# A two-layer network on one core: modulation chunks spread between the memory's products, and the attention queries' inverse root mean square put onto the scores

## The chip, the cores and the metric

The kernel runs on one core of one Trainium2 chip. It is one program that computes a whole small network from inputs in device memory. The metric is the device time of one execution in microseconds; the median of several executions is compared. The engines that matter are TensorE (PE in the profile, its weight loads PEld), VectorE (DVE), ScalarE (ACT) and SyncE (SP), whose one task here is to start the loads of the weights. A second DMA queue is fed by ScalarE.

## The reference, cut to what matters

256 latent tokens and 256 context tokens of 2048 features go through a layer with retention (8 heads), a layer with attention (16 query heads, 4 key/value heads) and a last block, which also attends to a memory. All is float32.

```
h = modulate(rms_norm(x, gain), shift, scale)     # shift, scale, gate: silu(c) @ ada_w, per layer
# memory of the last block: keys and values are products of the normed memory input
k_mem, v_mem = split(rms_norm(mem, mem_gain) @ w_mem_kv_2)
# layer 0, per head: q, k, v, g = h @ w_in ; retention ; finish(o, g) @ w_out
# layer 1:
q_l = rms_norm(heads(h @ w_q, 16, 128), q_gain)   # x * rsqrt(mean(x^2) + eps) * gain
q_l, k_l = rope_2d(q_l, row, col), rope_2d(k_l, row, col)
s = einsum(q_l, k) * scale + mask                 # over latent and context keys
y = (softmax(s, sink) @ v * silu(g)) @ w_out
```

## The kernel before, in words

**The weights.** Every weight comes from device memory once, in 936 chunks of 512 KB ([128, 1024] float32). Their order is written out by `stream_order` (L123). SyncE issues one DMA per chunk (L479) into a ring of raw slots: eight up to the first head of layer 0 (chunk 104), four from there. It issues the next one into a slot as soon as the slot's last chunk is consumed.

**Two kinds of chunk.** A *product chunk* is split in two parts: ScalarE writes `w_hi`, a rounded copy (L932), VectorE writes `w_lo = raw - w_hi` (L1413), which frees the raw slot. The product with activations, split in the same way, is three matmuls each (`product`, L506 to L508). Four pairs of `w_hi`, `w_lo` exist. A *modulation chunk* (a part of `ada_w`) is read by TensorE straight from its raw slot (L559), four chunks to a group of 256 columns of a layer's modulation; its slot is free when TensorE is done. After the fourth chunk ScalarE copies the sums out of PSUM (`ada_part`, L962), TensorE turns them (`ada_turn`, L575) and VectorE writes `mod` (`ada_add`, L1440, L1443).

**The look-ahead.** `weights_to(c)` on ScalarE and on VectorE splits up to four product chunks ahead of chunk `c`, in the order of the stream, and not past a slot whose modulation chunk comes later than `c`. ScalarE waits in it, in its own order, for the chunk's DMA and for the matmuls of four splits before.

**The order of the start.** (1) Modulation groups 0, 8, 1, 9 of layer 0. (2) `mk`: eight tiles of the memory's keys, two chunks each; after every second tile a modulation group (2, 10, 3, 11). (3) `mv`: two times eight chunks of the memory's values, with groups 4 and 12 in the first eight. (4) Groups 5 and 13, back to back. (5) `v(0)`: the value product of head 0, eight chunks of two k tiles, with the groups 6, 14, 7, 15 after its first four. For `v(0)` ScalarE and VectorE make the normed and modulated input of layer 0 on the way (`h_raws`, `h_parts`, `h_lows`), two k tiles per chunk, each of which needs the shift and scale of its group. The memory's input is normed likewise ahead of `mk`: a root and a reciprocal (`rstd`, L970, L1452), then for 16 k tiles `s_ctx` (L1546, VectorE), `h_hi` (L1028, ScalarE), `h_lo` (L1550, VectorE). (6) The heads of layer 0, with modulation chunks at each of their places by `modulation_beside`: two per place in head 0, one in the others.

**Other loads.** ScalarE's queue carries the tables (513 KB) and the memory's input (four of 512 KB) first, the tokens (four of 1 MB) at 17.8 us, and after `mv` it writes keys and values of the memory back to device memory (two of 1 MB, L1057, L1058).

**The attention.** Per key/value group (`kv`, 0 to 3) TensorE makes the gates (`az`), the scores of four heads (L738), transposes and values (L748, L757), the output product (`attn_out`), and in between the four query tiles of the next group (`aq`). The norm of a pair of query tiles is one chain: VectorE copies both tiles out of PSUM (L1724), ScalarE squares them (L1149), TensorE averages over the 128 features with a matrix of ones (L727, 512 columns), which leaves the mean in every partition, ScalarE takes the root (L970), VectorE the reciprocal of [128, 512] (L1729) and the product with gain and query (L1731); then comes the rotation (L1472 to L1475) with a swapped copy by ScalarE (L1003, L1004). VectorE adds the mask to the scores (L1752), takes the maximum (L1758), and ScalarE exponentiates.

Of the kernel before, what the change touches and what calls it, by code (L numbers as in the profile page):

```python
# [46 lines left out]
def columns(sizes):  # L47
# [16 lines left out]
def shape_constants():  # L64
# [10 lines left out]
    put("sum_parts", np.stack([p % 32 == 0, p % 32 == 1], 1))  # L75
# [25 lines left out]
def modulation_beside(h):  # L101


    places = [("t", i) for i in range(8)] + [("v", i) for i in range(8) if h < RET_HEADS - 1] + [("end",)]
    groups = [(0, n) for n in range(16, 24)] if h == 0 else [(1, n) for n in range(3 * h - 3, min(3 * h, 20))]
    chunks = [(layer, n, c) for layer, n in groups for c in range(4)]
    out, ended = {}, []
    for place in places:
        now = [chunks.pop(0) for _ in range(min(2 if h == 0 else 1, len(chunks)))]
# [6 lines left out]
BESIDE = [modulation_beside(h) for h in range(RET_HEADS)]  # L116


FIRST_GROUPS, MEM_GROUPS, LAST_GROUPS = (0, 8, 1, 9), (2, 10, 3, 11), (5, 13)
MV_GROUPS, V_GROUPS = ({3: 4, 7: 12}, {}), {0: 6, 1: 14, 2: 7, 3: 15}  # L120


def stream_order():  # L123
# [18 lines left out]
    for i in range(4):  # L142
        tile(("mk", 2 * i), "w_mem_kv_2", 2 * i * P)
        tile(("mk", 2 * i + 1), "w_mem_kv_2", (2 * i + 1) * P)
        ada(0, MEM_GROUPS[i])
    for n in range(2):
        for c in range(8):
            values(("mv", n), "w_mem_kv_2", W_M + n * 512, c)
            if c in MV_GROUPS[n]:
                ada(0, MV_GROUPS[n][c])  # L150
    for n in LAST_GROUPS:
        ada(0, n)
    for c in range(8):
        values(("v", 0), "ret_w_in", 2 * RET_Q, c)
        if c in V_GROUPS:
            ada(0, V_GROUPS[c])
# [19 lines left out]
    for c in range(8):  # L176
        values(("av",), "attn_w_in", q_w + kv_w, c)
    for h in range(GROUP):
        tile(("aq", 0, h), "attn_w_in", h * P)
    for i in range(ATTN_KV):  # L180
        tile(("ak", i), "attn_w_in", q_w + i * P)
# [90 lines left out]
class Banks:  # L272
# [42 lines left out]
    "v_set", "sink_set", "shifted", "sink_exp", "exped", "probs", "p_turned", "pv", "y_hi", "y_lo",  # L315
# [21 lines left out]
class Memory:  # L337


    def __init__(self, nc, ctx):  # L340
# [81 lines left out]
        self.sinks = sb("a_sinks", [P, GROUP])  # L422
        self.h_t1 = [self.a_s[i // 2][:, i % 2, :] for i in range(4)]
# [65 lines left out]
def tensor_program(nc, m, s):  # L489
    pe = nc.tensor  # L490
    banks = s.banks
    ident, ones_parts = m.table("ident"), m.table("sum_parts")
# [102 lines left out]
    pe.wait_ge(*s["tables_set"].at())  # L595
    ada_turn(0, 0)
    mean("mem", SIDE)
    ada(0, 1)
    ada_turn(0, 8)
    ada(0, 9)  # L600
# [1411 lines left out]
```

## Time and profile before

| | |
|---|---|
| runs | 3493.48, 3493.75, 3502.49 us; median 3493.75 |
| profiled execution | 3492.97 us, span 3491.7 us |
| TensorE busy | 3264.7 us, 93% of the span, 20298 matmuls |
| VectorE busy | 1738.8 us, 50% |
| ScalarE busy | 1260.3 us, 36% |
| DMA | 508.93 MB, mean 146 GB/s |
| places | `mk` from 61.6 us, `mv` from 117.4, `v(0)` from 190.2, head 0 from 259.0, head 1 in its `v` phase at about 440; query and key tiles of the attention 1944 to 2014, its four groups from 2038 |

Read the table as follows. TensorE is busy for most of the span, so what can be won is its idle time and the time in which its clock is granted at less than full speed. The page shows both by slices of 87 us:

```profile
PE   5979999999999999999997988987999999999998
PEclk9989999999999999999998999998999999999999
DMA  7753433333332333323243324443545444466654
```

The first three slices are the start, with TensorE idle for half of the first; the slices 23 to 27 are the attention.

### The profile page before, as it was taken

How to read it: one execution, taken by the hardware profiler on the slowest of the kernel's cores; microseconds unless marked ns; L12 is line 12 of the kernel's file. 1: busy time of each engine (PE TensorE's matmuls, PEld its weight loads, DVE VectorE, ACT ScalarE, POOL GpSimd, SP SyncE). 2: the span in 40 equal slices, each digit the busy share in tenths (PEclk: the TensorE clock that was granted, in tenths of full speed). 3: DMA queues.
4: the chain of work that ended last, by engine and by line, in shares of the span. 5: the costliest groups of instructions: out<-in, count | busy, mean ns of one | idle time of the engine just before them, and what ended most of it. 6: DMA issues, size and time to landing. Idle time of an engine off the chain costs nothing.

```text
span 3491.7 us, 47726 instructions
## 1 busy us (share of the span) xinstructions
PE 3264.7 (93%) x20298; PEld 2782.5 (80%) x20298; DVE 1738.8 (50%) x2491; ACT 1260.3 (36%) x1779; POOL 0.2 (0%) x4
## 2 busy tenths in 40 slices
PE   5979999999999999999997988987999999999998
PEld 3757677777777777777866878876999998999998
DVE  4533243434334343433436667766666555555555
ACT  3432222222222222222224454444554444444443
POOL 0000000000000000000000000000000000000000
PEclk9989999999999999999998999998999999999999
DMA  7753433333332333323243324443545444466654
GB/s 302 285 186 145 171 117 116 105 127 121 109 129 101 109 103 127 127 103 133 97 144 122 115 97 133 133 133 115 172 148 167 151 150 165 151 196 194 195 188 151
DMA packets 141635, 508.93 MB, mean 146 GB/s; under 512 B 15344, under 2 KB 19568, under 8 KB 140656
## 3 DMA queue, kind: packets, MB, share of 16 engines
q1 hardware_dynamic: 137040, 493.03, 41.5%
q10 hardware_dynamic: 4384, 12.85, 1.0%
q8 instruction: 161, 2.64, 0.3%
q14 instruction: 50, 0.41, 0.0%
HBM read 501.62 MB, written 4.19 MB: 145 GB/s over the span
## 4 chain that ended last, share of the span: by engine, by line
PE 85%; DVE 6%; DMA 3%; ACT 3%; issue 2%; SPq 0%; ACTq 0%; DVEq 0%
PE bank L506 26%; PE bank L508 25%; PE bank L507 25%; DMA raw<-stream 3%; PE bank L559 2%; PE bank L672 2%; DVE w_lo L1413 1%; PE bank L757 1%; PE bank L738 1%; PE bank L658 1%; PE bank L674 1%; DVE a_rstd L1729 1%; ACT a_s L1169 1%; PE bank L748 0%; ACT w_hi L932 0%
## 5 line engine op out<-in xcount | busy, mean ns | idle before, releaser
L506 PE MATMUL bank<-h_hi,w_hi 128*128 128x256 f32 (+1 forms) x4032 | 1269.0, 315 | 23.9 <-DVE w_lo L1413 21.6
L1413 DVE TENSOR_TENSOR w_lo<-raw,w_hi 128x1024 fp32r<-128x1024 f32 x744 | 901.5, 1223 | 695.5 <-ACT w_hi L932 690.6
L507 PE MATMUL bank<-h_lo,w_hi 128*128 128x256 f32 (+1 forms) x4032 | 1244.7, 309 | 0.0
L508 PE MATMUL bank<-h_hi,w_lo 128*128 128x256 f32 (+1 forms) x4032 | 1244.7, 309 | 0.0
L932 ACT ACTIVATE w_hi<-raw 128x1024 fp32r<-128x1024 f32 x744 | 779.1, 1057 | 1059.5 <-PE bank L508 601.5
L506 PEld LDWEIGHTS bank<-h_hi,w_hi 128*128 128x128 f32 x4032 | 762.5, 189 | 92.5 <-issue 36.8
L507 PEld LDWEIGHTS bank<-h_lo,w_hi 128*128 128x128 f32 x4032 | 763.4, 189 | 46.6 <-issue 4.9
L508 PEld LDWEIGHTS bank<-h_hi,w_lo 128*128 128x128 f32 x4032 | 761.2, 189 | 43.6
L506 PE MATMUL bank<-w_hi,h_hi 128*128 128x512 f32 x704 | 288.4, 410 | 44.9 <-DVE w_lo L1413 40.6
L508 PE MATMUL bank<-w_hi,h_lo 128*128 128x512 f32 x704 | 279.5, 397 | 0.0
L507 PE MATMUL bank<-w_lo,h_hi 128*128 128x512 f32 x704 | 279.0, 396 | 0.0
L1603 DVE SCALAR_TENSOR_TENSOR res<-bank,mod,res 128x256 f32<-128x256 f32 x320 | 134.1, 478 | 167.9 <-PE bank L508 167.9
L506 PE MATMUL bank<-o_hi,w_hi 128*128 128x512 f32 x512 | 201.6, 394 | 10.1 <-ACT vg L992 8.3
L506 PEld LDWEIGHTS bank<-w_hi,h_hi 128*128 128x128 f32 x704 | 135.1, 192 | 88.2 <-issue 51.8
L507 PE MATMUL bank<-o_lo,w_hi 128*128 128x512 f32 x512 | 200.5, 392 | 0.0
L508 PE MATMUL bank<-o_hi,w_lo 128*128 128x512 f32 x512 | 200.5, 392 | 0.0
L508 PEld LDWEIGHTS bank<-w_hi,h_lo 128*128 128x128 f32 x704 | 134.6, 191 | 29.6
L507 PEld LDWEIGHTS bank<-w_lo,h_hi 128*128 128x128 f32 x704 | 135.0, 192 | 29.0 <-issue 1.7
L559 PE MATMUL bank<-raw,cond 128*32 128x256 f32 x1536 | 119.6, 413 | 32.8 <-DMA raw<-stream 32.8
L506 PEld LDWEIGHTS bank<-o_hi,w_hi 128*128 128x128 f32 x512 | 97.0, 189 | 32.5 <-issue 12.5
L507 PEld LDWEIGHTS bank<-o_lo,w_hi 128*128 128x128 f32 x512 | 97.0, 190 | 20.0
L508 PEld LDWEIGHTS bank<-o_hi,w_lo 128*128 128x128 f32 x512 | 96.8, 189 | 20.3
(215 smaller groups left out, 2698.5 us busy)
## 6 DMA issues: line engine op xcount, KB each, us to landing
raw<-stream SPq DMA_DIRECT2D x936, 512.0 KB, 4.2
res<-tokens_in ACTq DMA_DIRECT2D x4, 1024.0 KB, 13.7
vg<-mem_in ACTq DMA_DIRECT2D x4, 512.0 KB, 10.7
res<-mem_kv ACTq DMA_DIRECT2D x2, 1024.0 KB, 10.0
out<-res SPq DMA_DIRECT2D x4, 512.0 KB, 3.0
mem_kv<-qk ACTq DMA_DIRECT2D x1, 1024.0 KB, 7.8
mem_kv<-vg ACTq DMA_DIRECT2D x1, 1024.0 KB, 11.1
tab<-tables ACTq DMA_DIRECT2D x1, 513.0 KB, 4.3
```

The lines of the kernel that those rows point to most:

```text
L506: pe.matmul(out, sh, mh, start=start, stop=False)
L507: pe.matmul(out, sh, ml, start=False, stop=False)
L508: return pe.matmul(out, sl, mh, start=False, stop=stop)
L559: mm = pe.matmul(out[32 * j:32 * j + 32, 0:L], m.cond[:, 4 * c + j, :], m.raw[SLOT[chunk]][:, j * L:(j + 1) * L], start=c == 0, stop=c == 3)
L658: mm = pe.matmul(outs[mt][:, :], m.qk[:, 2 + dt, L + mt * P:L + (mt + 1) * P], m.qk[:, dt, :], start=dt == 0, stop=dt == 1)
L672: pe.matmul(out[:, :], m.v[:, 2 + mt, dv], m.s_ctx[:, mt, :], start=mt == 0, stop=mt == 1)
L674: mm = pe.matmul(out[:, LAT], m.v[:, mt, dv], m.s_lat[:, mt, :], start=False, stop=mt == 1, skip_group_check=True)
L738: mm = pe.matmul(out[:, at - a0:at - a0 + n], q[:, qs], k, start=i == 0, stop=i == len(pairs) - 1)
L757: mm = pe.matmul(out[:, LAT], v, pt[:, kt, :], start=kt == 0, stop=kt == len(tiles) - 1)
L932: act.activation(m.w_hi[n % SLOTS][:, :], m.raw[SLOT[raw]][:, :], ACT.Copy).then_inc(s.hi, 1)
L1413: dve.tensor_tensor(m.w_lo[slot][:, :], m.raw[SLOT[raw]][:, :], m.w_hi[slot][:, :].bitcast(F32), ALU.subtract).then_inc(s.lo, 1)
L1603: i = dve.scalar_tensor_tensor(out=m.res[:, tile, cols], in0=psum(*what)[:, cols], scalar=m.mod[layer][:, 2 * KT + tile, side:side + 1], i ...
```

## The change

It has two parts that do not touch each other.

**The start.** `modulation_beside` now takes a list of places with a count of chunks at each, and the start uses it too: only the groups 0 and 8 come ahead of `mk`; the other 14 groups (56 chunks) lie two, three or five at a time behind each tile of `mk`, each second chunk of `mv` and the first five chunks of `v(0)`, so that no four chunks of a group need be neighbours. Head 0 has its 32 chunks nearly as before, the last place now without one. The small matrix `sum_parts`, which `ada_turn` needs, moves from the tables into the parameters, and the tables, the rotation of layer 0 and both writes of the memory (3 MB in all with them) are issued by ScalarE in `v(0)` behind its third chunk (c = 2). The tokens are issued one MB at a time. VectorE no longer has `ada_add(0, 8)` between the memory's `rstd` and its first `s_ctx`. In `v(0)`, `weights_to` comes ahead of `h_parts` (ScalarE) and `h_lows` (VectorE). In the heads, `o_rstd`'s reciprocal and the normed output stand one place apart (c = 1, c = 2).

**The attention.** The key tiles come ahead of the query tiles of group 0. The queries' norm is taken apart: VectorE multiplies each query tile by the gain as it leaves PSUM (`q_in`), ScalarE squares the tile from PSUM (`q_square`), the rotation follows at once. `q_means` is eight matmuls per group, each with the squares of 128 tokens of a head as the stationary side and one column of ones as the moving side, so that the means lie with a token per partition, [128, 8] for all four heads; root and reciprocal are taken of that. The result is multiplied onto the scores of the token, in the instruction that adds the mask. For group 0 these stand behind its gates, for the others in the third pair of `attn_out` of the group before. ScalarE loads its function tables 30 times where it was 28, the two more in group 0.

```diff
-FIRST_GROUPS, MEM_GROUPS, LAST_GROUPS = (0, 8, 1, 9), (2, 10, 3, 11), (5, 13)
-MV_GROUPS, V_GROUPS = ({3: 4, 7: 12}, {}), {0: 6, 1: 14, 2: 7, 3: 15}
+FIRST_GROUPS = (0, 8)
+BESIDE = {"start": modulation_beside(
+    [(("mk", i), n) for i, n in enumerate((2, 2, 3, 2, 3, 2, 2, 3))]
+    + [(("mv", i // 4, 2 * (i % 4) + 1), n) for i, n in enumerate((2, 2, 3, 2, 2, 3, 2, 5))]
+    + [(("v", i), n) for i, n in enumerate((4, 3, 3, 3, 3, 0, 0, 0))],
+    [(0, n) for i in range(1, 8) for n in (i, 8 + i)])}
...
@@ tensor_program
-    pe.wait_ge(*s["tables_set"].at())
...
+    for n in range(8):
+        tile(("mk", n), SIDE)
+        beside("start", "mk", n)
...
-    for n in LAST_GROUPS:
-        ada(0, n)
...
         values_chunk(("v", 0), outs, c)
+        beside("start", "v", c)
...
+    def q_means(kv):
+        out = bank("q_mean", kv)
+        pe.wait_ge(*banks.at("aq", kv, GROUP - 1))
+        for h in range(GROUP):
+            for qt in range(2):
+                at = h % 2 * L + qt * P
+                mm = pe.matmul(out[:, 2 * h + qt:2 * h + qt + 1], m.nsq[h // 2][:, at:at + P], m.ones_head[:, 0:1],
+                               start=True, stop=True)
+        mm.then_inc(*s["q_meaned"].up(kv))
...
-        if not last:
-            norm(("aq", kv + 1, 0), 0)
...
+            if n == 2 and not last:
+                q_means(kv + 1)
@@ scalar_program
     for c in range(8):
+        weights_to(WHERE["v", 0][c])
...
             h_parts(0, 2 * c + 2, m.h_t0)
             h_parts(0, 2 * c + 3, m.h_t0)
-        weights_to(WHERE["v", 0][c])
...
+        if c == 2:
+            act.dma_start(m.tab[:, :], d["tables"]).then_inc(s.load["tab"], 16)
...
+    def q_square(kv, h):
+        act.wait_ge(*s["q_in"].at(kv, h))
+        at = h % 2 * L
+        act.activation(m.nsq[h // 2][:, at:at + L], psum("aq", kv, h)[:, LAT], ACT.Square).then_inc(*banks.up("aq", kv, h))
@@ vector_program
     reciprocal(("mean", "mem"), m.rstd[:, SIDE], ("mem",))
-    ada_add(0, 8)
...
+    def q_in(kv, h):
+        ahead(("aq", kv, h))
+        done(("aq", kv, h))
+        dve.tensor_scalar(m.a_q[:, h, :], psum("aq", kv, h)[:, LAT], m.gains[:, 0:1], None, ALU.mult
+                          ).then_inc(*s["q_in"].up(kv, h))
...
+                    i = dve.scalar_tensor_tensor(out=here, in0=scored, scalar=rstd[:, qt:qt + 1], in1=mask[:, qt, a0:a1],
+                                                 op0=ALU.mult, op1=ALU.add)
...
         if not last:
-            q_norm(kv + 1, 0)
+            q_rotate(kv + 1, 0)
```

**ScalarE between the memory's root and `mk`.** `part` is the copy of `ada_part`, `rstd` the memory's root, `h_hi` the rounded input of the memory. Before:

```order
L962 ACTIVATE part<-bank 128x256 x2
L970 ACT_TABLE_LOAD
L970 ACTIVATE rstd<-bank,eps 128x256
L932 ACTIVATE w_hi<-raw 128x1024 x3
L962 ACTIVATE part<-bank 128x256
L1028 ACTIVATE h_hi<-s_ctx 128x256 x8
L932 ACTIVATE w_hi<-raw 128x1024
```

After:

```order
L959 ACTIVATE rstd<-bank,eps 128x256
L1009 DMA res<-tokens_in 128x2048
L921 ACTIVATE w_hi<-raw_71 128x1024
L921 ACTIVATE w_hi<-raw_72 128x1024
L951 ACTIVATE part<-bank 128x256
L1023 ACTIVATE h_hi<-s_ctx 128x256 x16
L921 ACTIVATE w_hi<-raw 128x1024 x2
```

The three splits ahead of the first `h_hi` were of the chunks 16 to 18 of the stream and are now two, of chunks 12 and 13 (the splits of 8 and 9 stand ahead of the root).

**VectorE in `v(0)`, around one chunk.** `h_lo` is the lower part of the chunk's input, `decay` and `s_ctx` are where the next input is made, `mod` is `ada_add`. Before:

```order
L1465 TENSOR_TENSOR h_lo<-s_ctx,h_hi 128x512 x2
L1459 TENSOR_TENSOR decay<-res,rstd 128x512 x2
L1413 TENSOR_TENSOR w_lo<-raw,w_hi 128x1024
L1443 TENSOR_SCALAR mod<-bank,par 128x2 x2
L1465 TENSOR_TENSOR h_lo<-decay,h_hi 128x512 x2
```

After:

```order
L1429 TENSOR_TENSOR w_lo<-raw_72,w_hi 128x1024
L1481 TENSOR_TENSOR h_lo<-s_ctx,h_hi 128x512 x2
L1475 TENSOR_TENSOR decay<-res,rstd 128x512 x2
L1459 TENSOR_SCALAR mod<-bank,par 128x2 x2
L1429 TENSOR_TENSOR w_lo<-raw,w_hi 128x1024
```

`w_lo` has moved ahead of `h_lo` and the next raw inputs.

**VectorE at a pair of query tiles.** `a_q` holds the queries, `a_rstd` what the norm made and later the swapped copy. Before:

```order
L1413 TENSOR_TENSOR w_lo<-raw,w_hi 128x1024 x2
L1724 COPY a_q<-bank 128x256
L1778 SCALAR_TENSOR_TENSOR a_g<-bank,a_g 128x256
L1781 TENSOR_TENSOR a_o_lo<-a_g,a_o_hi 128x256
L1729 RECIPROCAL a_rstd_81<-a_rstd_81 128x512
L1731 SCALAR_TENSOR_TENSOR a_q<-a_q,a_gains,a_rstd_81 128x512
L1472 TENSOR_TENSOR a_q<-a_q,a_rope 128x512
```

After:

```order
L1429 TENSOR_TENSOR w_lo<-raw,w_hi 128x1024 x2
L1748 TENSOR_SCALAR a_q<-bank,a_gains 128x256
L1803 SCALAR_TENSOR_TENSOR a_g<-bank,a_g 128x256
L1806 TENSOR_TENSOR a_o_lo<-a_g,a_o_hi 128x256
L1488 TENSOR_TENSOR a_q<-a_q,a_rope 128x512
```

The reciprocal and the product behind it are gone from between `a_o_lo` and the rotation; the copy has become a product with the gain.

## Rows read from the trace of the kernel before

**Rows 1.** Page: shares of the chain that ended last.
```profile
PE 85%; DVE 6%; DMA 3%; ACT 3%; issue 2%; SPq 0%; ACTq 0%; DVEq 0%
```

**Rows 2.** Windows (us, busy PE, PEld, DVE, ACT, POOL; PEclk, DMA share, GB/s).
```profile
61.50:117.40 55.90, 55.84 (x528) 51.63 (x528) 31.73 (x46) 24.93 (x35) 0.00 (x0) 1.00 0.70 265
117.40:168.00 50.60, 50.60 (x278) 39.48 (x274) 25.11 (x28) 19.86 (x27) 0.00 (x0) 1.00 0.77 290
168.00:190.20 22.20, 3.66 (x66) 2.00 (x65) 5.09 (x8) 5.81 (x10) 0.00 (x0) 0.63 0.73 284
190.20:259.00 68.80, 59.38 (x344) 46.31 (x345) 27.51 (x44) 29.78 (x49) 0.00 (x0) 0.92 0.47 169
2013.70:2037.70 24.00, 15.30 (x101) 13.83 (x100) 16.41 (x17) 11.40 (x18) 0.00 (x0) 0.79 0.25 87
2124.60:2223.40 98.80, 89.06 (x663) 81.49 (x662) 69.03 (x103) 47.97 (x75) 0.00 (x0) 0.97 0.41 128
```

**Rows 3.** Waits of TensorE from 0 to 260 us (us, times, longest).
```profile
PE bank L506 <- DVE w_lo L1413: 37.3, 4, 18.5
PE bank L559 <- DMA raw<-stream: 25.0, 15, 8.0
```

**Rows 4.** Timeline ahead of the first memory product (start, us, engine).
```profile
24.82 1.75 DVE L1452 RECIPROCAL rstd<-rstd 128x256 f32<-128x256 f32 x1 [1.15 <-ACT rstd L970]
...
37.07 0.47 DVE L1440 TENSOR_SCALAR mod<-bank,bias,par 128x2 f32<-128x2 f32 x2 [10.50 <-PE bank L575]
...
45.35 1.06 ACT L932 ACTIVATE w_hi<-raw 128x1024 fp32r<-128x1024 f32 x1 [20.56 <-DMA raw<-stream]
...
49.13 1.32 ACT L1028 ACTIVATE h_hi<-s_ctx 128x256 fp32r<-128x256 f32 x4
...
61.56 0.55 PE L506 MATMUL bank<-h_hi,w_hi 128*128 128x256 f32 x1 [11.26 <-DVE w_lo L1413]
```

**Rows 5.** Chain that ended last, in order of time (start, us, what).
```profile
68.63 0.34 PE bank L575 x4
...
74.73 1.86 PE bank L559 x32
...
199.65 4.41 DMA raw<-stream
```

**Rows 6.** Timeline before and in `v(0)`.
```profile
184.52 1.06 ACT L932 ACTIVATE w_hi<-raw 128x1024 fp32r<-128x1024 f32 x1 [10.57 <-DMA raw<-stream]
...
204.08 1.06 ACT L932 ACTIVATE w_hi<-raw 128x1024 fp32r<-128x1024 f32 x1 [17.19 <-DMA raw<-stream]
...
208.73 0.69 DVE L1465 TENSOR_TENSOR h_lo<-s_ctx,h_hi 128x512 fp32r<-128x512 f32 x1 [0.95 <-ACT h_hi L984]
...
211.90 0.77 PE L506 MATMUL bank<-w_hi,h_hi 128*128 128x512 f32 x1 [3.57 <-DVE w_lo L1413]
```

**Rows 7.** Waits of TensorE in the value product beside head 0, 376 to 441 us.
```profile
PE bank L506 <- DVE w_lo L1413: 5.1, 3, 3.4
PE bank L575 <- ACT part L962: 4.4, 1, 4.4
```

**Rows 8.** Waits of TensorE in the attention, 2013 to 2323 us.
```profile
PE bank L506 <- DVE w_lo L1413: 18.4, 7, 8.0
PE bank L727 <- ACT a_sq L1149: 17.3, 7, 3.1
```

**Rows 9.** VectorE's groups, 2013 to 2323 us (count | busy, mean ns | idle before).
```profile
L1729 DVE RECIPROCAL a_rstd<-a_rstd 128x512 f32<-128x512 f32 x8 | 26.8, 3352 | 14.8 <-ACT a_rstd L970 14.8
...
L1752 DVE TENSOR_TENSOR a_s<-bank,a_mask 128x512 f32<-128x512 f32 x24 | 15.7, 685 | 0.6 <-PE bank L738 0.5
...
L1731 DVE SCALAR_TENSOR_TENSOR a_q<-a_q,a_gains,a_rstd 128x512 f32<-128x512 f32 x6 | 4.5, 751 | 0.2
```

**Rows 10.** Timeline of ScalarE at a root of the attention.
```profile
2077.67 1.28 ACT L970 ACT_TABLE_LOAD   x1
2078.96 0.69 ACT L970 ACTIVATE a_rstd<-bank,eps 128x512 f32<-128x512 f32 x1
```

More of the change, by code:

```diff
@@ L141, in stream_order @@
         ada(0, n)
[L142 to L145, printed above, removed]
+    for n in range(8):
+        tile(("mk", n), "w_mem_kv_2", n * P)
+        beside("start", "mk", n)
     for n in range(2):
@@ L594, in tensor_program @@
     ada(0, 8)
-    pe.wait_ge(*s["tables_set"].at())
     ada_turn(0, 0)
     mean("mem", SIDE)
-    ada(0, 1)
     ada_turn(0, 8)
-    ada(0, 9)
-    ada_turn(0, 1)
-    before = 9
-    for i in range(4):
-        tile(("mk", 2 * i), SIDE)
-        ada_turn(0, before)
-        tile(("mk", 2 * i + 1), SIDE)
-        ada(0, MEM_GROUPS[i])
-        before = MEM_GROUPS[i]
+    for n in range(8):
+        tile(("mk", n), SIDE)
+        beside("start", "mk", n)
     for n in range(2):
@@ L769, in tensor_program @@
         norm(("ak", n - 1), (n - 1) % 2)
+    tile(("aq", 0, 0), LAT)
     norm(("ak", ATTN_KV - 1), (ATTN_KV - 1) % 2)
+    for h in range(1, GROUP):
+        tile(("aq", 0, h), LAT)
     for kv in range(ATTN_KV):
@@ L1029, in scalar_program @@
         if k == 7:
-            ada_part(0, 9)
-    for i in range(4):
-        for j in range(2):
-            ahead(("mk", 2 * i + j))
-            if j == 0:
-                act.wait_ge(s.load[f"tok{i}"], 16)
-            for k in (4 * i + 2 * j, 4 * i + 2 * j + 1):
-                square("x0", k, (sq_out(k, BOTH), m.res[:, k, :]))
-        ada_part(0, MEM_GROUPS[i])
+            weights_to(WHERE["mk", 0][0], 1)
+    for n in range(8):
+        ahead(("mk", n))
+        if n % 2:
+            if n < 7:
+                tokens_in((n + 1) // 2)
+        if n:
+            x0_squares(n - 1)
+        beside("start", "mk", n)
     for n in range(2):
@@ L1581, in vector_program @@
                 h_raws(0, 1, m.h_t0)
+            beside("start", "mv", n, c)
+            if n == 0 and c == 3:
+                reciprocal(("mean", "x0"), m.rstd[:, :], ("x0",))
     h_lows(0, 0, m.h_t0)
     for c in range(8):
+        weights_to(WHERE["v", 0][c])
         if c < 7:
@@ L1589, in vector_program @@
             h_raws(0, c + 2, m.h_t0)
-        weights_to(WHERE["v", 0][c])
-        if c == 0:
-            for n in LAST_GROUPS:
-                ada_add(0, n)
-        if c - 1 in V_GROUPS:
-            ada_add(0, V_GROUPS[c - 1])
+        beside("start", "v", c)
+    dve.wait_ge(s.load["tab"], 16)
     dve.wait_ge(s.load["kv_out"], 32)
@@ L1685, in vector_program @@
             ahead(("ada", 1, 20), 4)
+            reciprocal(("o_mean", h), m.o_rstd[:, :], ("o", h))
             normed_of_head()
@@ L1838, in vector_program @@
                 add_out(("attn_out", kv, n, j), 2 * n + j, (0,), 1)
+            if n == 2 and not last:
+                q_reciprocal(kv + 1)
             if last:
```

245 lines of the change are left out of this document (120 added, 125 removed).

## The prediction

> **What bounds the kernel now.** I read the chain that ended last by engine first. 85% of it is TensorE [rows 1], so instructions off TensorE's path cost nothing by themselves, and the change must be valued by idle time of TensorE and by its granted clock. The windows show where those are. `mk` and `mv` are full: 55.84 busy of 55.90 us and 50.60 of 50.60 [rows 2]. What lies around them is not: between `mv` and `v(0)` TensorE is busy 3.66 of 22.20 us, in `v(0)` 59.38 of 68.80 at a clock of 0.92, in an attention group 89.06 of 98.80 at 0.97 [rows 2]. The waits say on what: up to 260 us, 37.3 us for `w_lo` in four waits and 25.0 us for chunks of the modulation [rows 3]. While `mk` and `mv` run full the DMA engines are busy 0.70 and 0.77 of the time, and 265 GB/s at 0.70 are 379 GB/s at a full share, or 1.38 us for a chunk of 524 kB. So the start has phases in which TensorE has all the work and others in which the DMAs have it. The attention's waits are 18.4 us for `w_lo` and 17.3 for the squares of the norms [rows 8].
>
> **The start, up to `mk`.** Before, ScalarE waited 20.56 us in its order for chunk 16, up to 45.35, and only then made the first `h_hi` at 49.13 [rows 4]; VectorE stood 10.50 us before `ada_add(0, 8)` [rows 4] ahead of its first `s_ctx`. The product chunks that ScalarE now waits for ahead of the first `h_hi` are 8, 9, 12 and 13 of the stream. The reciprocal ended at 26.57 [rows 4]; I put it at 28.6, 2 us later, since the root now stands behind the splits of 8 and 9. From the first `h_hi` to TensorE's first product were 12.4 us for 16 k tiles (61.56 less 49.13, [rows 4]). The new first `h_hi` at about 30, the four `s_ctx` that were ready before now inside (1.7), give the last `h_lo` and the second half's `w_lo` at about 44, and `mk`'s first tile ends 3 us later, at 47. It ended at 68.6 [rows 5]. That is 21.6 us, of which the modulation chunks taken out from before it must be paid back later.
>
> **`mk` and `mv`.** `mk` was 55.9 us. Less the first tile (68.63 less 61.56, 7.1) and four groups of four chunks at 1.86 [rows 5] 41.4 remain for seven tiles with their turns. Now 19 modulation chunks at 1.86 / 4 = 0.465 lie there, 8.8. `mk` ends at 47 + 41.4 + 8.8 = 97.2. `mv` was 50.6 with two groups (3.7); 46.9 and 21 chunks (9.8) and one turn more (0.34 by [rows 5], 0.45 with its weight loads) are 57.1: it ends at 154.3. Do the DMAs keep up? From the first tile's end to head 0 about 98 chunks' worth is to be moved, tokens and the memory's 3 MB included: 98 x 1.38 = 135 us, to 182, ahead of TensorE. Within `mk` it is nearly even: two tiles with 4.75 chunks are about 14 us of TensorE, and 8.75 chunks with the megabyte of tokens at every second tile about 14 us of DMA. I add nothing there and keep up to 8 us for the range.
>
> **`v(0)`.** The 18.5 us of the bridge are gone with groups 5 and 13. The products, turns and low clock are 59.38 less 7.4 of modulation = 52.0; 16 chunks (7.4) give 59.4. The clock of 0.92 cost 5.5 us of 68.8; with fewer and shorter waits I take 2.5, so 56.4. Waits stay, since a place's input still needs `mod` of a group that just ended. Before, the chunk landed 4.41 after TensorE was done [rows 5], and from the split at 204.08 to the end of `h_lo` at 209.42 were 5.3 us [rows 6]: 9.7 from one to the other, where TensorE now has 5.6 of product and 1.86 of modulation, 7.45. Four places at 2.25 are 9. Putting `w_lo` first saves the 1.2 us of it behind `h_lo`, and is in this. The 3 MB that now move inside `v(0)` are six chunks' time, 8 us; in the old place ScalarE waited 10.57 us for a chunk just behind those writes [rows 6]. I take 5 and keep 0 to 10. With 3 us for copies and turns not ready in time, `v(0)` ends at 154.3 + 56.4 + 9 + 5 + 3 = 227.7. It ended at 259.0: 31.3 us less. Bounds: 20 (`mk` bound by DMA 8, the writes 10 in place of 5), 51 (no waits and full clock in `v(0)`).
>
> For the writes the Trainium skill bears on this ("DMA: Bandwidth & Descriptors", section "Issuing engines are not separate DMA queues"): DMAs of ScalarE and of SyncE run on the same 16 engines and interleave, so the second queue gives no room of its own. The wait of 10.57 us agrees. By it alone the writes cost the stream their full 8 us, and the sum would be 3 us less gain.
>
> **Head 0.** Its value phase waits 5.1 + 4.4 = 9.5 us [rows 7], the 4.4 for the last group's copy at the end. That place has no chunk now, and the reciprocal of `o_rstd` no longer stands ahead of a `w_lo` together with the normed output. I leave 3 of the 9.5 (the tile places with three chunks in four slots) and gain 7 with a little clock. Bounds 2 and 11.
>
> **The attention.** Per query pair, VectorE loses a reciprocal of 3.35 us and a product of 0.75 [rows 9], and TensorE's wait for the squares goes. That wait and the one for `w_lo` behind the chain were 35.7 us over 310 us [rows 8]; in one whole group TensorE stood 98.80 - 89.06 = 9.7 us [rows 2]. What is late next: `o_lo` ahead of `attn_out`, whose chain of values, gate and copy is unchanged; it is about 2.8 of the 9.7, and 0.5 of small ones stays. So 6.4 us of waits go per group. The clock of 0.97 costs 3.0 us per group; I take 2.2 of them back. TensorE's own work: two norm products of 512 columns go, about 0.77 each by the nearest row [rows 6], 1.5; eight of one column come. A turn's two small matmuls are 0.34 [rows 5], so eight are 1.4, and twice that at most if their weight loads show. Net -0.1 to +1.3; I set +0.5. That is 6.4 + 2.2 - 0.5 = 8.1 per group, 24.3 for the three groups that prepare the next. VectorE's product of a scalar with the scores and the mask has no row of its own. The lower bound is the addition alone at 0.685, the upper one the reciprocal's 3.35; the same kind at the same shape is L1731 at 0.751 [rows 9], and I take that: 32 x 0.07 = 2.2 us on VectorE, of which some 0.5 on the path (the score's chain stands behind other heads' work). The multiplication of the query tile by its gain replaces a copy of the same shape, at nothing, between -0.1 and +0.1 each. Ahead of group 0 the wait of 8.0 us [rows 8] comes from two key norms in a row, which stay as they are; the key tiles move ahead of the query tiles, but the new squares now stand behind `q_in(0, 0)`, which stands behind a key norm. I find 8.1 us of waits for 8.7 and 1.4 of the clock's (0.79, [rows 2]), 2 us. Two more table loads of 1.28 [rows 10] fall beside group 0's gates and are covered but for about 0.5. Sum: 24.3 + 2 - 0.5 - 0.5, about 26. Bounds 15 (4 per group) and 36 (11 per group).
>
> The root stands 0.01 us behind the load's end [rows 10]. The Trainium skill ("ScalarE: Activation LUTs", section "What ACT_TABLE_LOAD costs") adds a drain of about 1.38 us to each switch. By that the two loads would be 5.3 us and not 2.6, and with the cover here the sum would be up to 2.7 us less gain. No such gap stands between these two rows.
>
> **The sum.** 31 + 7 + 26 = 64 us. From the profiled execution's 3492.97, which is 0.8 us below the median, comes 3429.
>
> **The rivals.**
> - *The start only moves its hunger.* The share of 0.73 that the bridge had [rows 2] comes back inside `mk`, where tokens and three chunks meet, and `v(0)` still waits for landings. Speaks for it: 0.70 and 0.77 already before, with fewer chunks. Against: the sum of 135 us in 180. Then the start gives 10: 3493 - 43 = 3450. 12%.
> - *ScalarE takes the place of the norms.* Squares from PSUM, swap and the split stand in one order on ScalarE; if `w_hi` becomes late by what the norm was, a group gives under 3 and the attention 8: 3447. For it: 14.8 us of VectorE's wait for the root was ScalarE's [rows 9]. Against: ScalarE is busy 47.97 of 98.80 [rows 2]. 11%.
> - *All covers hold.* `v(0)` waits for nothing, the groups give 10: 3407. 12%.
> - *Slower: the look-ahead blocks.* ScalarE's split runs up to eight chunks ahead in the stream once modulation chunks lie between, and waits there in its own order while the square or the copy that TensorE needs stands behind. In `v(0)` the wait of 3.57 us [rows 6] with 2 us of clock is that kind: 5.7 us. If each of the 16 places of the memory's products had it, it would cost 91 us and the start would be 60 longer than before: 3493 + 60 - 33 = 3520. It decides from 64 / 16 = 4.0 us per place. Against: 0.06 us of idle time in 55.9 [rows 2], with the same look-ahead. 3%.
>
> **How the numbers follow.** The forecast, 62%. Its own bounds are 20 to 51, 2 to 11 and 15 to 36, which are not met together; 3405 to 3458 takes in both rivals that give less and most of the better case. A measurement tells 0.3%, about 10.5 us, from no change. Faster by more needs only one of three parts: 0.95. Within it 0.02, slower 0.03.
>
> **What would show it.** The first memory product at about 36 us and no `w_hi` wait over 5 us before it; `mk` and `mv` full, ended near 97 and 154; head 0 begun near 228, with waits of about 2 us in `v(0)`; no reciprocal of [128, 512] among the queries; a period of about 90.5 us in place of 98.7 for an attention group, with one wait ahead of `attn_out` left. It would be wrong if `mk` shows TensorE waiting for `w_lo` at its tiles, or if the wait ahead of the scores or of `attn_out` grows by what the norms gave up.

## The result and the profile after

| | median us | runs | ratio to before, 95% interval |
|---|---|---|---|
| before | 3493.75 | 3492.56 to 3502.49 | |
| changed | 3462.32 | 3454.88 to 3469.64 | 0.9902 (0.9881 to 0.9924) |

The kernel is 31 us faster where 64 were forecast; 3462 lies outside the range 3405 to 3458. The profiled execution has a span of 3461.0 us. By stages it tells where the gain is missing:

| stage | before | after | gain | forecast |
|---|---|---|---|---|
| head 0 begins at | 259.0 | 256.8 | 2.2 | 31 |
| head 0, to its output product | 181.2 | 177.5 | 3.7 | 7 |
| heads and the rest of layer 0, to the query and key tiles (1943.65, now 1935.91) | 1503.4 | 1501.6 | 1.8 | 0 |
| from there to the end of the span | 1548.0 | 1525.1 | 22.9 | 26 |

The windows of the changed kernel for the stages of [rows 2] (same columns): `mk`, `mv`, all from the end of `mv` to head 0, the end of the key and query tiles, and an attention group.

```profile
36.10:104.30 68.20, 62.24 (x553) 55.05 (x553) 37.06 (x60) 26.35 (x41) 0.00 (x0) 0.96 0.77 295
104.30:169.10 64.80, 60.97 (x382) 45.00 (x378) 26.57 (x35) 18.93 (x25) 0.00 (x0) 0.94 0.78 283
169.10:256.80 87.70, 61.10 (x344) 47.34 (x345) 33.43 (x51) 38.43 (x66) 0.00 (x0) 0.84 0.52 198
...
1997.80:2027.80 30.00, 24.85 (x193) 24.62 (x193) 17.88 (x25) 19.64 (x29) 0.00 (x0) 0.89 0.37 126
2120.50:2210.60 90.10, 86.73 (x674) 81.42 (x673) 62.10 (x100) 47.55 (x76) 0.00 (x0) 1.00 0.41 141
```

`mk` now begins at 36.1, 25.5 us early. Less of this lead was to be left at the end of `mv` in any case, since modulation chunks have moved into `mk` and `mv`: the forecast had 154.3 there, and it came at 169.1, so 14.8 us of the 29.1 that head 0 is late (256.8 against 227.7) are lost by then. The third line holds the other 14.3: 87.7 us, where the forecast had 73.4, 26.6 of them idle and the clock at 0.84. TensorE's waits up to head 0, against [rows 3]:

```profile
PE bank L510 <- DVE h_lo L1481: 20.6, 2, 13.7
PE bank L563 <- DMA raw<-stream: 12.9, 8, 8.8
PE bank L579 <- ACT part L951: 9.3, 4, 3.0
PE bank L510 <- DVE w_lo L1429: 8.2, 2, 5.6
PE bank L510 <- ACT vg L981: 6.0, 1, 6.0
PE bank L510 <- issue: 3.8, 1, 3.8
```

The longest are no longer for weights (`w_lo`), as they were before, but for the input (`h_lo`). The two are these, at the third and the fifth chunk of `v(0)`:

```profile
200.18 0.80 PE L510 MATMUL bank<-w_hi,h_hi 128*128 128x512 f32 x1 [6.90 <-DVE h_lo L1481]
...
230.31 0.79 PE L510 MATMUL bank<-w_hi,h_hi 128*128 128x512 f32 x1 [13.68 <-DVE h_lo L1481]
```

ScalarE and VectorE ahead of the second, the fifth chunk of `v(0)`:

```profile
200.84 1.06 ACT L921 ACTIVATE w_hi<-raw 128x1024 fp32r<-128x1024 f32 x1 [1.44 <-DMA raw<-stream]
...
225.19 1.06 ACT L921 ACTIVATE w_hi<-raw 128x1024 fp32r<-128x1024 f32 x1 [16.43 <-DMA raw<-stream]
226.15 1.08 ACT L968 ACTIVATE s_ctx<-s_ctx,mod 128x256 f32<-128x256 f32 x2
227.26 0.63 ACT L973 ACTIVATE h_hi<-s_ctx 128x512 fp32r<-128x512 f32 x1
...
201.92 1.23 DVE L1429 TENSOR_TENSOR w_lo<-raw,w_hi 128x1024 fp32r<-128x1024 f32 x1 [0.34 <-ACT w_hi L921]
...
226.28 1.23 DVE L1429 TENSOR_TENSOR w_lo<-raw,w_hi 128x1024 fp32r<-128x1024 f32 x1 [19.17 <-ACT w_hi L921]
...
229.57 0.69 DVE L1481 TENSOR_TENSOR h_lo<-s_ctx,h_hi 128x512 fp32r<-128x512 f32 x1 [0.95 <-ACT h_hi L973]
```

Counting the splits of the stream, 200.84 is the fifth chunk and 225.19 the sixth. The fifth chunk's weights were complete at 203.2, 27 us before TensorE began on them. What it lacked was the input, and ScalarE made it only when the split in front of it, of the *sixth* chunk, had its data. The chain shows how long chunks were on the way there:

```profile
186.38 8.64 DMA raw<-stream
...
209.70 15.47 DMA raw<-stream
```

8.64 and 15.47 us, where [rows 5] had 4.41. Part of this is the place in the bunch: the 4.41 was the second of five chunks that left SyncE within 2 us, while 8.64 is the last of five (184.6 to 186.4) and 15.47 the last of four, beside the 3 MB of ScalarE's queue (208.4 to 210.3). The forecast took 4.41 for every place.

In the attention, VectorE's groups against [rows 9], for 2004 to 2300 us:

```profile
L1776 DVE SCALAR_TENSOR_TENSOR a_s<-bank,a_q_rstd,a_mask 128x512 f32<-128x512 f32 x24 | 17.0, 744 | 0.3
L1748 DVE TENSOR_SCALAR a_q<-bank,a_gains 128x256 f32<-128x256 f32 x15 | 7.2, 478 | 0.0
...
L1758 DVE RECIPROCAL a_q_rstd<-a_q_rstd 128x8 f32<-128x8 f32 x4 | 0.8, 194 | 1.2 <-ACT a_q_rstd L1172 1.2
```

The reciprocal is 0.194 us in place of 3.35, the addition with a product 0.744 in place of 0.685 (0.751 was taken). TensorE's waits there, against [rows 8]:

```profile
PE bank L510 <- DVE a_o_lo L1806: 7.2, 3, 3.0
PE bank L510 <- DVE w_lo L1429: 5.1, 1, 5.1
PE bank L738 <- issue: 3.2, 3, 1.9
PE bank L729 <- DVE a_s L1796: 1.2, 1, 1.2
```

### The profile page after: what moved, and what is told of

The parts are those of the page before. It is cut to its first block, busy times and chain, and to the rows that moved or that the text cites. A ratio compares the mean times of both kernels' runs of the same rounds, so it can differ in the third digit from the quotient of the medians.

```text
span 3461.0 us, 47818 instructions
## 1 busy us (share of the span) xinstructions
PE 3266.4 (94%) x20346; PEld 2791.9 (81%) x20346; DVE 1710.4 (49%) x2479; ACT 1260.8 (36%) x1785; POOL 0.2 (0%) x4
## 4 chain that ended last, share of the span: by engine, by line
PE 88%; DVE 4%; DMA 3%; ACT 3%; issue 2%; SPq 0%; ACTq 0%; DVEq 0%
PE bank L510 26%; PE bank L512 26%; PE bank L511 26%; DMA raw<-stream 3%; PE bank L563 2%; PE bank L653 2%; PE bank L719 1%; PE bank L738 1%; DVE w_lo L1429 1%; PE bank L639 1%; PE bank L655 1%; PE bank L729 1%; ACT a_s L1185 0%; ACT w_hi L921 0%; PE bank L579 0%
```

## The experiments

Unchanged stages differ by up to 15 us between executions (last section), so the start's experiments are compared by their profiles. Each kernel has one profiled execution, and its start has a spread of its own. The changed kernel, start_only, writes_c0, h_first and h_both do the same work in the same order up to the first product of `v(0)`, and they reach it at 169.2 to 175.1 us. From there to head 0 the changed kernel and start_only, whose `v(0)` is the same, both take 81.7 us. The length of `v(0)` is therefore the sharper measure for an edit inside it, and of the begin of head 0 up to 6 us can be chance:

| kernel | first product of `v(0)` | from it to head 0 | head 0 begins | median us | ratio to before (95%) |
|---|---|---|---|---|---|
| changed | 175.1 | 81.7 | 256.8 | 3462.3 | 0.9902 (0.9881 to 0.9924) |
| attn_only | 191.7 | 68.1 | 259.7 | 3473.1 | 0.9941 (0.9920 to 0.9961) |
| start_only | 172.4 | 81.7 | 254.1 | 3484.5 | 0.9965 (0.9951 to 0.9978) |
| h_first | 172.5 | 79.8 | 252.3 | 3457.9 | 0.9893 (0.9862 to 0.9923) |
| h_both | 171.4 | 70.0 | 241.4 | 3448.0 | 0.9856 (0.9834 to 0.9878) |
| writes_before | 173.9 | 73.1 | 247.0 | 3464.1 | 0.9908 (0.9880 to 0.9937) |
| writes_c0 | 169.2 | 74.9 | 244.1 | 3453.4 | 0.9875 (0.9860 to 0.9890) |
| spread8 | 177.3 | 74.1 | 251.4 | 3467.8 | 0.9910 (0.9886 to 0.9933) |
| h_both_writes | 175.9 | 61.7 | 237.6 | 3446.0 | 0.9853 (0.9834 to 0.9872) |
| even | 192.3 | 45.9 | 238.2 | 3448.4 | 0.9866 (0.9847 to 0.9885) |
| ring6 | 179.6 | 72.4 | 252.0 | 3463.7 | 0.9895 (0.9866 to 0.9923) |
| ring10 | 159.9 | 70.3 | 230.3 | 3438.3 | 0.9835 (0.9811 to 0.9859) |
| before10 | 174.3 | 65.7 | 239.9 | 3477.0 | 0.9937 (0.9912 to 0.9962) |
| even10 | 178.3 | 46.5 | 224.8 | 3438.0 | 0.9826 (0.9801 to 0.9851) |
| best10 | 174.5 | 55.0 | 229.5 | 3434.7 | 0.9816 (0.9793 to 0.9840) |
| ring10_h_both | 160.3 | 65.6 | 225.9 | 3432.9 | 0.9811 (0.9794 to 0.9828) |
| final10 | 173.0 | 46.9 | 219.9 | 3432.4 | 0.9810 (0.9782 to 0.9837) |

**The two parts apart.** attn_only is the kernel before with the attention's edits; start_only is the changed kernel without them.

```diff
-    tile(("aq", 0, 0), LAT)
...
+    def q_means(kv):
```

> The attention part alone, on the start and heads of before. The changed kernel gained 31.4 us of medians; its profile puts 22.9 us of that behind the key and query tiles (1548.0 to 1525.1 us from there to the end), 3 to 6 in the heads and 2 in the start. If the parts are additive, this run is 22 to 25 us under before, 3469 to 3472, with a group's period near 90.1 us. If the attention's gain leans on the new order of the stream, or the start of the changed kernel had in fact gained more and the attention less, it gains under 15.

> The change without its attention part: start and heads as changed, the queries' norm as before. Additive parts give a gain of 6 to 10 us, 3484 to 3488, and head 0 begins near 257 us where it was 259 before. By the forecast's own terms (31 + 7) it would be 3455. A gain over 20 would mean that the attention part disturbs the rest.

The gains are 0.6% and 0.35% of 3497.65, the median of before beside them, 21 and 12 us by the ratios, and add up to the changed kernel's 34 (0.98%) within their intervals. The parts don't touch each other, and the attention is the larger one (3473.1, a microsecond over what was expected). start_only came out at 3484, where the forecast's own terms made it 3455: nearly all of the error is there (29 of some 33 us, by the stages above).

**The order in `v(0)`.** h_first puts ScalarE's order back, h_both VectorE's too.

```diff
@@ scalar_program (h_first and h_both)
-        weights_to(WHERE["v", 0][c])
...
             h_parts(0, 2 * c + 2, m.h_t0)
             h_parts(0, 2 * c + 3, m.h_t0)
+        weights_to(WHERE["v", 0][c])
@@ vector_program (h_both)
-        weights_to(WHERE["v", 0][c])
...
             h_raws(0, c + 2, m.h_t0)
+        weights_to(WHERE["v", 0][c])
```

> The changed kernel with ScalarE's order in v(0) put back: the next chunk's inputs (h_parts) ahead of weights_to, as before the change; the order of VectorE is left as changed. Theory of the order: the split that ScalarE waits for stands ahead of the inputs that TensorE needs, so from the chunk's landing to TensorE's start are 5.1 us (195.05 to 200.18 in the changed kernel); with the inputs made while it waits, 2.5 us less at each of the three waits in v(0), 6 to 8 us faster. Theory of the ring: the landing sets the wait and the order moves only the 2.5 us behind it, and where VectorE's order is against it, less: 0 to 6 us faster. Slower than the changed kernel by over 3 us would mean that the split is what TensorE waits for.

> The changed kernel with the order of v(0) put back on both engines: ScalarE makes the next chunk's inputs ahead of weights_to, and VectorE makes h_lows and h_raws ahead of it. With ScalarE's order alone the two waits were 3.9 and 11.9 us. Theory of the order: in the changed kernel the weights of the fifth chunk were split at 201.9 us, 28 us before TensorE began it at 230.3; it waited for inputs that stood behind the split of the sixth chunk, which landed at 225.2. VectorE has the same look-ahead in front of h_lows. With both put back the wait of 6.9 us at c = 2 falls under 2, the one of 13.7 at c = 4 goes and a smaller one of 4 to 7 appears at c = 5, where the landing itself is what is missing: head 0 begins at 240 to 246 in place of 256.8. Theory of the landing alone: waits of 10 or more at c = 4 stay, head 0 at 250 or later.

ScalarE alone: 6.90 became 3.88 and 13.68 became 11.87, and `v(0)` is 1.9 us shorter. That looked as if the landing decided, and was misleading: VectorE's `w_lo` of the later chunk stood ahead of `h_lo` in the same way. With both put back head 0 begins at 241.4, 15.4 us earlier. Of these, 11.7 lie in `v(0)` (81.7 to 70.0); the other 3.7 come ahead of its first product, where nothing was edited. h_both's two longest waits inside `v(0)`:

```profile
191.63 0.47 PE L510 MATMUL bank<-w_hi,h_hi 128*128 128x512 f32 x1 [2.29 <-DVE w_lo L1429]
...
219.49 0.78 PE L579 MATMUL bank<-par,part 128*128 128x2 f32 x3 [5.96 <-ACT part L951]
```

The fifth chunk has no wait now, and what comes later is of the size expected (4 to 7). The sixth chunk, which had taken 15.47 us, is as late as before; only its split waits for it, on ScalarE, with the inputs made ahead of it:

```profile
204.34 0.63 ACT L973 ACTIVATE h_hi<-s_ctx 128x512 fp32r<-128x512 f32 x1
216.48 1.06 ACT L921 ACTIVATE w_hi<-raw 128x1024 fp32r<-128x1024 f32 x1 [11.50 <-DMA raw<-stream]
```

In the chain stands the chunk behind it, with most of its time hidden:

```profile
180.65 3.12 DMA raw<-stream
...
207.02 10.97 DMA raw<-stream
```

So the order is what turned late chunks into waits, 11.7 us of `v(0)`. The forecast had credited it with a saving of 1.2 us.

**The transfers of ScalarE's queue.** writes_before undoes their move, writes_c0 issues all four two chunks earlier, spread8 sets them apart, h_both_writes joins writes_before and h_both.

```diff
@@ scalar_program, v(0) (writes_c0)
-        if c == 2:
+        if c == 0:
             act.dma_start(m.tab[:, :], d["tables"]).then_inc(s.load["tab"], 16)
@@ scalar_program, behind mv (writes_before)
+    act.wait_ge(*banks.at("mk", 7))
+    act.dma_start(d["mem_kv"][:, 0:8, :], m.mem_k).then_inc(s.load["kv_out"], 16)
+    act.wait_ge(*banks.at("mv", 1, 1))
@@ scalar_program, v(0) (spread8; the keys are written in mv)
-        if c == 2:
+        if c == 0:
+            act.wait_ge(*banks.at("mv", 1, 1))
...
+        if c == 3:
+            act.dma_start(m.tab[:, :], d["tables"]).then_inc(s.load["tab"], 16)
```

> The changed kernel with the four transfers of ScalarE's queue in v(0) (tables, rotation, both writes of the memory) issued two chunks earlier, behind chunk 0 (c = 0) in place of c = 2. Theory 1, the 3 MB collide: at c = 2 they are issued in the same moment as five chunks and hold up the chunk of c = 4, the wait of 13.7 us; behind c = 0 the DMA engines stood idle for some 7 us (their share was 0.43 in the ten us from 180), so the wait falls to about 6 and the kernel gains 5 to 8 us. Theory 2, the ring of slots sets it: the wait of c = 4 is there whatever else moves, like the 6.9 us of c = 2, and the kernel gains under 2 us, or the wait only moves to c = 2.

> The changed kernel with this one part undone: the tables are loaded first of all, the rotation with the tokens, and both writes of the memory are issued at the end of mv, as before the change. Theory of the collision: the wait of 13.7 us at v(0)'s fifth chunk falls to 3 to 7, but the writes now meet the chunks that v(0) opens with, as they did before (10.57 us), and that wait grows by 4 to 8; in sum head 0 begins 0 to 6 us earlier than the 256.8 of the changed kernel. Rival, that the stall at the fifth chunk is the ring's and not the writes': it stays over 10 us, and head 0 begins later than 260.

> The changed kernel with the four transfers apart: the memory's keys are written during mv (behind its fourth chunk), the values behind v(0)'s first chunk, the tables are loaded behind its fourth and the rotation behind its sixth. Collision: no transfer of over 1 MB meets a bunch of chunks; the wait of 13.7 us falls under 4, head 0 begins at 240 to 246 and the kernel is 10 to 16 us faster than the changed one. Ring: the bunches of v(0) still cost 6 to 7 us at the third chunk and as much at the fifth; head 0 at 249 or later, under 8 us faster.

> The same, and the four transfers of ScalarE's queue where they were before the change. Writes alone put back began head 0 at 247.0, with waits of 5.3 and 5.9 us in v(0). If order and writes are two separate causes, both go: no wait over 2 us inside v(0), head 0 begins at 236 to 240. If they are one cause seen twice, this is no earlier than the better of the two alone.

In writes_before the wait of 13.68 is 5.94, and the transfer behind it has half its length, against the 15.47 above:

```profile
184.75 7.03 DMA raw<-stream
...
206.91 7.73 DMA raw<-stream
```

The collision is 7.7 us of this wait, and 8.6 of `v(0)` (81.7 to 73.1); the opening of `v(0)`, which was expected to grow by it, waits 5.8, as in the changed kernel (6.0). Its median does not follow the 9.8 us of head 0: its four runs lie between 3455 and 3472, and such a spread can't tell it from the changed kernel. spread8 met the poorer of its two expectations (head 0 at 249 or later): the values' write, 1 MB by itself, met the next bunch, and the wait of the third chunk rose from 6.9 to 8.9:

```profile
187.84 10.59 DMA raw<-stream
...
213.33 7.08 DMA raw<-stream
```

writes_c0 did better than hoped at the fifth chunk, which does not wait at all, by moving the load between bunches; 3.3 us of wait came up at the fourth. Its median is 8.9 us under the changed kernel's, where 5 to 8 were expected. With the order right, the writes are worth 8.3 us of `v(0)` (70.0 to 61.7, no wait over 2.3 us inside it). That is as much as without it (8.6), and both together give 20.0: order and writes are two causes, as the first expectation of h_both_writes had it. Head 0 begins only 3.8 us earlier than in h_both (237.6), because `v(0)` was reached 4.5 later. Up to there TensorE waits 10.9 us for `part`, against 5.7 in h_both, and the tables and the rotation are loaded in this stretch again. That these loads are the reason is not shown: the changed kernel, without them, waits 9.3, and 4.5 us is within what the same start differs by.

**No modulation chunks in `v(0)`.**

```diff
-    [(("mk", i), n) for i, n in enumerate((2, 2, 3, 2, 3, 2, 2, 3))]
-    + [(("mv", i // 4, 2 * (i % 4) + 1), n) for i, n in enumerate((2, 2, 3, 2, 2, 3, 2, 5))]
-    + [(("v", i), n) for i, n in enumerate((4, 3, 3, 3, 3, 0, 0, 0))],
+    [(("mk", i), n) for i, n in enumerate((3, 3, 3, 3, 3, 3, 3, 3))]
+    + [(("mv", i // 4, 2 * (i % 4) + 1), n) for i, n in enumerate((4, 4, 4, 4, 4, 4, 4, 4))]
+    + [(("v", i), n) for i, n in enumerate((0, 0, 0, 0, 0, 0, 0, 0))],
```

> The changed kernel with all 56 modulation chunks of the start beside mk and mv (three behind each of the eight tiles, four behind each second chunk of mv), none in v(0), which before had 16. Theory of the ring: a modulation chunk holds its slot until TensorE reaches it, so in v(0) the next product chunks are issued late and in a bunch; without them v(0) has no wait at c = 2 and c = 4 beyond the writes, takes 50 to 58 us in place of 87.7, and mk and mv take 16 chunks of 0.465 more and waits of 5 to 10 us for DMA: 15 to 20 us faster than the changed kernel. Rival, total DMA time: the start is bound by the sum of transfers, so what v(0) wins is lost as waits for chunks in mk and mv, and the time is within 4 us of the changed kernel.

As the first theory had it: `v(0)` takes 46 us from its first product (192.3 to 238.2) and has no wait behind it, and `mk` and `mv` wait in small pieces for `part`. From 100 us to head 0:

```profile
PE bank L579 <- ACT part L951: 9.2, 7, 1.9
```

The DMA engines' total was no bound: head 0 begins 18.6 us earlier with the same bytes.

**The ring of raw slots.** The one line in three kernels, with the slots' memory to it (ring10 and before10 also move the rotation's load, and ring10 one early split, as its expectation says):

```diff
-WIDE = 8
+WIDE = 10
```

> The changed kernel with six raw slots before the first head in place of eight, and nothing else. Theory of the ring: each place's chunks are issued later by two chunks' worth, some 2 to 3 us at each of the 24 places where DMA is near the bound; v(0) and mv wait more, 25 to 60 us slower than the changed kernel. Rival, total DMA time: the engines carry the same bytes and the time stays within 8 us.

> The changed kernel with ten raw slots before the first head (the two more lie where the heads' rotation table and small buffers are later; the rotation table's load moves behind v(0)'s sixth chunk for that, and one early split of VectorE moves behind the memory's mean). Theory of the ring: the waits of 6.9 us at c = 2 and part of 6.0 at c = 0 and 3.8 in mv go, 8 to 15 us faster than the changed kernel. Rival, the writes of 3 MB: the wait of 13.7 at c = 4 stays near 10 or more, and the gain is under 5. Total DMA time: no change.

> The kernel before with ten raw slots in place of eight up to the first head (the rotation's load moves behind v(0)'s sixth chunk for that). If slots alone are what the start lacks, the bridge of 18.5 us ahead of v(0) shrinks by the two more chunks that are there early, and head 0 begins 5 to 12 us before 259. If the bunches of four modulation chunks at one place and their order hold it (the groups 5 and 13 back to back empty the ring whatever its size), it begins at 255 or later, and the gain of ring10 over the changed kernel (26 us in head 0's begin) is one of both together.

Ten slots gave more than expected, 26.5 us of head 0's begin: `v(0)` is reached 15.2 us earlier (at 159.9, where no kernel with eight slots and the changed places is ahead of 169.2) and is 11.4 shorter. Six did not cost what the theory said: `v(0)` is reached 4.5 us later, but is 9.3 shorter. The chunks that it waited for stood third, second and second among those issued together, where the changed kernel's stood last; two of the three transfers are short:

```profile
189.48 6.11 DMA raw<-stream
198.72 5.37 DMA raw<-stream
216.41 10.79 DMA raw<-stream
```

So "fewer slots, later issue" alone is refuted. That the place in the bunch makes up for it is read from these rows; no run changes it alone. The time of ring6 is what its rival, the DMA engines' total, had foretold, but even and ring10 refute that one. before10 went past both of its expectations: slots help the old order too, by 19.1 us, so most of ring10's gain is no merit of interleaving.

**Put together.** even10 is even with ten slots, ring10_h_both is ring10 with h_both's order, best10 and final10 add this to even10 (best10 also has h_first's order and spread8's transfers):

```diff
     def ada_part(layer, n):
-        ahead(("ada", layer, n), 4)
+        if layer or n % 8 == 0 or n >= 16:
+            ahead(("ada", layer, n), 4)
```

> Both together: ten slots and no modulation chunks in v(0). With eight slots this order began head 0 at 238.4 us with waits of 1.5 us at most places of mv for the copy of a group (ScalarE waits for a chunk in front of it). Theory of the ring: with two more slots these shrink, head 0 begins at 222 to 230, the kernel takes 3432 to 3440. If the DMA engines' total were the bound in mv, head 0 begins at 236 or later and the time is that of eight slots, 3448.

> Ten slots, no modulation chunks in v(0), the four transfers apart, ScalarE's inputs ahead of its splits in v(0), and ada_part of the start's later groups without its own look-ahead (by which ScalarE waits for a chunk of the tile after next before it copies the sums that TensorE's turn needs). Ten slots and the even order alone began head 0 at 224.8 us with 9.5 us of waits in mv and v(0) and 4.3 in mk. If the look-ahead in ada_part makes TensorE's waits for part, these six waits of 0.4 to 1.2 us go and head 0 begins at 217 to 221, 3430 to 3436 us. If the chunks' landing makes them, nothing changes: 224 to 226.

> Ten raw slots with the order of v(0) put back on both engines. Ten slots alone had waits of 2.7, 0.2, 1.5, 4.3 and 2.6 us in v(0) and began head 0 at 230.3. If those too are inputs behind a split that waits, they go: head 0 at 218 to 223. If the two more slots have already taken what the order costs, 228 or later.

> Ten slots, no modulation chunks in v(0), the order of the changed kernel, and ada_part of the start's later groups without its own look-ahead. Ten slots and the even order began head 0 at 224.8 with waits of TensorE for part of 0.4 to 1.2 us at seven places. The kernel that had this edit among four had none of these waits in mk and mv, but 6.6 and four of 1.7 us in v(0) by ScalarE's order there. Expected: head 0 at 219 to 223, and the median 3426 to 3436.

even10 is where the theory of the ring put it (head 0 at 224.8, 3438.0 us). ring10_h_both begins head 0 at 225.9, between its two expectations, with `v(0)` 4.7 us shorter than ring10's, where the order was worth 11.7 with eight slots: part of the order's cost was taken by the slots already. final10 has one wait left between 100 us and head 0, and its windows are near full:

```profile
PE bank L510 <- DVE h_lo L1484: 7.4, 1, 7.4
```

```profile
36.00:101.40 65.40, 62.89 (x597) 55.38 (x597) 34.88 (x60) 25.11 (x39) 0.00 (x0) 1.00 0.85 330
101.40:219.90 118.50, 111.14 (x683) 85.99 (x680) 61.57 (x84) 59.73 (x91) 0.00 (x0) 0.96 0.73 273
```

ScalarE's look-ahead in `ada_part` had made the waits for `part`: final10 differs from even10 by this edit alone, and of the 3.7 us that even10 waits for `part` from 100 us on it has none. best10 missed both of its expectations (217 to 221, or 224 to 226) with 229.5: in `v(0)` it has a wait of 6.6 and four of 1.7 us for `h_lo`. It has the half-turned order, ScalarE's inputs first and VectorE's weights first, and spread8's transfers besides, and no run takes the two apart. final10 beats both kernels: 0.9810 of before, some 30 us under the changed one. By the medians it can't be told from best10 and ring10_h_both.

## Why the prediction was wrong, point by point

- *`mk` first at 36, first tile done at 47*: 36.11 and 48.2. Right.
- *`mk` ended at 97, `mv` at 154*: 101.6 and 169.1. This is the first step that failed, 14.8 us: to "Do the DMAs keep up?" the answer was to add nothing and to keep 8 us for the range, with the clock at 1.00 as before. Missing were waits and low clock: 3.4 us of idle time at two turns, whose `part` stood behind ScalarE's look-ahead; 3.8 us and a slow product behind it (8.24 for 5.77) in `mv`. The clock was granted at 0.97 in `mk` and 0.92 in `mv`. I had added up the DMA time (135 us in 180). What fails is the assumption under this sum, that the DMAs run ahead freely. They stood nearly still while the ring was full (busy 0.35 of the time from 140 to 150 us) and then had to bring four or five chunks at once. That the ring's size sets this, ring10 shows: with two more slots `v(0)` is reached 15.2 us earlier, and from 110 to 160 us the DMA share is 0.85 and the clock 1.00. How the 14.8 us divide between single waits is not shown.
- *`v(0)`: four places at 2.25, writes 5, small ones 3*: 87.7 us against 73.4; 26.6 of it in three waits, and 6.2 of low clock in the products behind them (8.05, 7.57 and 7.82 for 5.76). This is the second step that failed, 14.3 us, and in it the sentence "Putting `w_lo` first saves the 1.2 us of it behind `h_lo`". The order saves 1.2 us only when the next splits have their data. `weights_to` splits up to four chunks ahead, so "`w_lo` first" meant "wait for a chunk needed one or two products later, and then make the input needed now". h_both measures it: 11.7 us of `v(0)`. The writes, taken at 5 with 0 to 10 kept, cost 8.3 to 8.6 (h_both_writes, writes_before). With both undone the stage is 66.4 us, a wait of 4.7 and 61.7 from the first product, and the forecast without its 5 for the writes was 68.4: the rest of the sum was sound in size.
- *Bounds and sums*: The lower bound of the start's gain was given as 20; its two terms, 8 and 5, lead from 31.3 to 18. The attention's terms add up to 25.3, not 26. Neither changes the forecast by more than 2 us, and the measured 2.2 of the start lies below both bounds.
- *The rival "the look-ahead blocks"* named the mechanism, but priced it at `mk` and `mv`, and at 3%, because there the trace of before showed no idle time. In the trace of before the inputs stood ahead of the look-ahead in `v(0)`; the change reversed just that. The forecast priced the moved instruction by its own duration.
- *The rival "the start only moves its hunger"*, a gain of 10, was nearest in size (2.2, and 4.9 in start_only), and half right: the DMAs did fall behind in `mk` and `mv`, though not by their total, and `v(0)` did wait, but for inputs.
- *Head 0: 7.* 3.7. The waits fell from 9.5 to 5.0, where 3 were to stay, and the longest of them, 3.5, stands at the head of the value product, where the first product then runs 8.44 us at the low clock in place of 5.84.
- *Attention: 26.* 22.9 with the rest of the program, 23.9 up to the fourth group. The two whole groups have 90.2 and 91.6 us (forecast 90.5), with one wait of 2.7 to 3.0 ahead of `attn_out`. Group 0 gave 5.0 and not 8.1: two waits of 1.2 and 1.9 us stand in its first part, the first of them for `a_s`, whose chain begins with the new root and reciprocal. Ahead of it 2.2 for 2. The eight small matmuls of `q_means` took 1.7 us, for 1.4 to 2.8. The two added table loads cost ScalarE their 1.28 us and no more: the load at 2026.20 begins where the gate's activation ends and is followed by the root at 2027.50. This agrees with [rows 10].

```profile
2024.51 1.28 ACT L986 ACT_TABLE_LOAD   x1
2025.80 0.39 ACT L986 ACTIVATE a_g<-bank 128x256 f32<-128x256 f32 x1
2026.20 1.28 ACT L1172 ACT_TABLE_LOAD   x1
2027.50 0.27 ACT L1172 ACTIVATE a_q_rstd<-bank,eps 128x8 f32<-128x8 f32 x1
```

## What to carry to other kernels

When a change moves a helper past other work on an engine that works in order, price all that the helper may wait for, its look-ahead above all, and not the duration of the instruction one has in mind; and if two engines have the same helper, move it on both or on none. The time of a DMA stream does not follow from its total alone: see where the ring is full, what leaves together when it opens, and which of the bunch is awaited. Undoing half of an order can show almost nothing, while the whole shows the cause. And before a difference is put down to an edit, see whether it lies behind the first edited instruction.

## What was not expected of the hardware

The granted clock does not tell all of TensorE's rate. In the last stage TensorE has no gap, the clock is granted at 1.00, and the code is the same in all kernels; still 350 us hold 3090 matmuls in one execution and 2974 in another. The changed kernel, spread8 and final10:

```profile
2990.00:3340.00 350.00, 350.00 (x3090) 350.00 (x3090) 198.43 (x233) 155.21 (x188) 0.00 (x0) 1.00 0.57 192
```

```profile
2984.00:3334.00 350.00, 350.00 (x2974) 350.00 (x2973) 192.80 (x226) 149.50 (x182) 0.00 (x0) 1.00 0.57 186
```

```profile
2953.00:3303.00 350.00, 350.00 (x3091) 350.00 (x3090) 199.04 (x235) 154.62 (x188) 0.00 (x0) 1.00 0.58 193
```

That is 3.8% and some 15 us over the stage, in spread8, even10 and h_first among the profiled executions. It is no matter of records missing from a trace: between the issues of the same two weight chunks (the stream's 800 and 850) lie 141.1 us in these three and 135.8 in all others. Among a kernel's runs there are steps of the same size (h_first: 3476.5 profiled, 3453.5 to 3461.0 otherwise); that they are this effect is not shown, as only one run of each has a trace. What sets it was not found.

A chunk of 512 KB that is the first of a bunch landed 3.1 to 5.6 us after its issue (seven bunches of the changed kernel, 130 to 200 us); the last of four to six issued within 3 us took 5.9 to 9.4, and 15.5 with 3 MB more. In `v(0)` of the changed kernel the last of a bunch was the one waited for.
